# Moving weight roundings behind other ScalarE work in two stages, and spreading VectorE's convolution taps differently

## The reference

```python
# first block, its feed-forward part (D_FF = 2816)
up = einsum('bld,df->blf', h, w_up)
a, b = split(up, 2)
acc = conv_b + sum(a_pad[:, j:j + L] * conv_w[j] for j in range(3))   # 3 taps
h += einsum('blf,fd->bld', silu(acc) * b, w_down)

# each of the two layers: half a SwiGLU, this mixer, half a SwiGLU
proj = u @ w_in                      # q, k, v, a, b, g_sb, g_conv
y_sb = stick_breaking_attention(q, k, v) @ w_attn_out
x = causal_conv(a * sigmoid(b), conv_w) + conv_b      # 31 taps, 512 channels
y_conv = silu(layernorm(x)) @ w_conv_out
m = sigmoid(g_sb) * y_sb + sigmoid(g_conv) * y_conv
h += m @ w_out
```

## Time and profile before

| | |
|---|---|
| median of three runs | 1551.68 us (1550.74 to 1555.36) |
| the profiled execution, its own time | 1551.68 us |
| its span, first to last instruction | 1549.8 us |
| PE busy | 1528.6 us (99%) |
| DVE busy | 1073.2 us (69%) |
| ACT busy | 757.2 us (49%) |
| POOL busy | 406.6 us (26%) |
| mean granted TensorE clock | 0.99 |

### The profile page before, as it was taken

The page is one execution under the profiler, slowest core; times in us unless marked ns, Lnnn a source line. Parts: engine busy times, 40 slices in busy tenths (PEclk is TensorE's granted clock), DMA queues, the critical chain, the costliest instruction groups (busy, mean ns, idle before and its releaser), DMA issues.

```text
span 1549.8 us, 31398 instructions
## 1 busy us (share of the span) xinstructions
PE 1528.6 (99%) x11612; PEld 1461.0 (94%) x11612; DVE 1073.2 (69%) x1686; ACT 757.2 (49%) x1072; POOL 406.6 (26%) x158
## 2 busy tenths in 40 slices
PE   8999999999999999999999999999999999999997
PEld 7778999989999999999999999999999999999986
DVE  6333888875865768987876553755547998887754
ACT  5333665555444435447644443544444446644442
POOL 4324100053444420000034343343420000044452
PEclk9889999999999999999999999999999999999999
DMA  7213456664555554434555564455644434556662
GB/s 242 84 64 90 133 172 189 204 211 135 172 184 184 183 154 152 137 116 148 166 174 179 186 194 149 163 176 173 214 146 133 150 122 150 181 172 178 198 222 94
DMA packets 65832, 250.91 MB, mean 162 GB/s; under 512 B 7520, under 2 KB 8800, under 8 KB 65760
## 3 DMA queue, kind: packets, MB, share of 16 engines
q1 hardware_dynamic: 65760, 249.92, 51.3%
HBM read 248.84 MB, written 1.05 MB: 161 GB/s over the span
## 4 chain that ended last, share of the span: by engine, by line
PE 94%; DVE 4%; issue 1%; ACT 1%; DMA 0%; SPq 0%; DVEq 0%; ACTq 0%
PE W L1284 25%; PE W L1286 24%; PE W L1285 24%; PE W L1354 5%; PE XP L1378 5%; PE W L1353 3%; PE X L1378 2%; PE W L1322 1%; PE W L1323 1%; PE W L1324 1%; DVE wlo L730 1%; DVE scr L1143 1%; DVE proj L747 0%; DMA raw<-in_w 0%; PE X L1301 0%
## 5 line engine op out<-in xcount | busy, mean ns | idle before, releaser
L1284 PE MATMUL W<-xh,whi 128*128 128x272 f32 (+2 forms) x2416 | 702.3, 291 | 2.8 <-DVE wlo L730 1.6
L346 POOL TENSOR_TENSOR wlo<-raw,whi 128x1024 fp32r<-128x1024 f32 (+1 forms) x152 | 405.7, 2670 | 1131.2 <-ACT whi L384 1131.2
L1286 PE MATMUL W<-xh,wlo 128*128 128x272 f32 (+2 forms) x2416 | 695.7, 288 | 0.0
L1285 PE MATMUL W<-xl,whi 128*128 128x272 f32 (+2 forms) x2416 | 693.9, 287 | 0.0
L384 ACT ACTIVATE whi<-raw 128x1024 fp32r<-128x1024 f32 (+1 forms) x439 | 483.7, 1109 | 162.4 <-PE W L1286 132.3
L1284 PEld LDWEIGHTS W<-xh,whi 128*128 128x128 f32 x2416 | 458.7, 190 | 8.7 <-issue 4.9
L1285 PEld LDWEIGHTS W<-xl,whi 128*128 128x128 f32 x2416 | 458.6, 190 | 0.2
L1286 PEld LDWEIGHTS W<-xh,wlo 128*128 128x128 f32 x2416 | 458.7, 190 | 0.0
L730 DVE TENSOR_TENSOR wlo<-raw,whi 128x1024 fp32r<-128x1024 f32 (+1 forms) x285 | 370.7, 1301 | 74.3 <-ACT whi L384 73.8
L1284 PE MATMUL W<-ax,whi 128*128 128x272 f32 (+2 forms) x816 | 234.9, 288 | 1.6 <-DVE ax L1125 1.2
L1286 PE MATMUL W<-ax,wlo 128*128 128x272 f32 (+2 forms) x816 | 234.3, 287 | 0.0
(11 more groups left out here) (194 smaller groups left out, 1218.6 us busy)
## 6 DMA issues: line engine op xcount, KB each, us to landing
raw<-in_w SPq DMA_DIRECT2D x359, 512.0 KB, 3.6
raw<-in_w SPq DMA_DIRECT2D x80, 704.0 KB, 4.1
h<-in_hT SPq DMA_DIRECT2D x4, 272.0 KB, 4.8
out<-h SPq DMA_DIRECT2D x4, 256.0 KB, 2.4
scr<-in_cst SPq DMA_DIRECT2D x1, 1000.0 KB, 9.3
cst<-in_cst SPq DMA_DIRECT2D x1, 472.0 KB, 6.8
prm<-in_prm SPq DMA_DIRECT2D x1, 180.0 KB, 8.9
m<-in_meta SPq DMA_DIRECT2D x1, 64.0 KB, 8.9
```

What stands on the lines that cost most here:

```text
L346: pool.tensor_tensor(wlo[:, j, 0:cols], raw[:, j, 0:cols], whi[:, j, 0:cols].bitcast(F32), ALU.subtract).then_inc(lo_ready[j], 1)
L1284: pe.matmul(out, whi[:, j, w], mh, start=start and k == 0, stop=False, skip_group_check=True)
L1285: pe.matmul(out, whi[:, j, w], ml, start=False, stop=False, skip_group_check=True)
L1286: ins = pe.matmul(out, wlo[:, j, w], mh, start=False, stop=stop and k == len(rhs) - 1, skip_group_check=True)
```

## The change

In `tap_plan`, steps 8 to 13 get three taps each (two before), and every fourth step from step 16 on gets one (two before). The total stays 120, so the last step, 29, gets six instead of eight.

In `ffn_up` with `conv`, ScalarE does the first tap of an even slab ahead of `hi_ahead` (behind it before). Without `conv` nothing is changed.

At the end of the mixer, each `hi_ahead` between the layer norm's square root and the output projection is moved one place back: the one of slab `ga + 1`, slot 1 goes behind the four roundings of L696, slot 2 behind the large `Sigmoid` (L700), and in the loop over j the slabs of the output projection's group are rounded one turn later. VectorE's and TensorE's code is the same but for the taps.

```diff
-        room = 0 if s < 2 else 3 if s < G_GLU else 2 if s < SB_FROM else (6, 5, 2, 10)[(s - SB_FROM) % 4]
+        room = 0 if s < 2 else 3 if s < SB_FROM else (6, 5, 1, 10)[(s - SB_FROM) % 4]
...
                     for j in range(4):
                         b, c = j // 2, 2 * i + j // 2
+                        if j % 2 == 0 and conv:
+
+                            act.wait_ge(evac_done, 4 * (g + i) + j + 1)
+                            act.activation(actv[:, b, t:], gate[:, b, t:T], ACT.Identity,
+                                           scale=prm[:, bass.ds(PRM_CW1 + CONV_W * c, 1)],
+                                           bias=prm[:, bass.ds(PRM_CB1 + c, 1)]).then_inc(cv_first, 1)
                         if not first:
                             hi_ahead(g + i, j, own, nxt)
                         elif j == 2:
                             hi_ahead(g + i, 3, own, nxt)
-                        if j % 2 == 0 and conv:
-
-                            act.wait_ge(evac_done, 4 * (g + i) + j + 1)
-                            act.activation(actv[:, b, t:], gate[:, b, t:T], ACT.Identity,
-                                           scale=prm[:, bass.ds(PRM_CW1 + CONV_W * c, 1)],
-                                           bias=prm[:, bass.ds(PRM_CB1 + c, 1)]).then_inc(cv_first, 1)
                         if j % 2 == 0:
                             if conv:
                                 act.wait_ge(conv_ready, c + 1)
...
-                hi_ahead(ga, 1, K8D, K8D)
+                hi_ahead(ga, 1, K8A, K8A)
                 for c in range(CC):
                     act.wait_ge(ln_norm, CC * l + c + 1)
                     act.activation(y[:, c, :], y[:, c, :], ACT.Silu, scale=prm[:, PRM_LNG + CC * l + c:PRM_LNG + CC * l + c + 1],
                                    bias=prm[:, PRM_LNB + CC * l + c:PRM_LNB + CC * l + c + 1]).then_inc(ln_silu, 1)
-                hi_ahead(ga, 2, K8D, K8D)
                 for c in range(CC):
                     act.wait_ge(ln_silu, CC * l + c + 1)
                     act.activation(ah[:, CC + c, :], y[:, c, :], ACT.Copy).then_inc(s_hi, 1)
-                hi_ahead(ga, 3, K8D, K8D)
+                hi_ahead(ga, 2, K8A, K8A)
                 act.preload_act_table_set("sigmoid_and_others")
                 act.wait_ge(evac_done, 4 * ga)
                 act.activation(proj[:, GCV:GCV + DC, t:], proj[:, GCV:GCV + DC, t:], ACT.Sigmoid).then_inc(sig_ready, 1)
-                hi_ahead(ga + 1, 0, K8D, K8D)
+                hi_ahead(ga, 3, K8A, K8A)
                 for j in range(4):
-                    if j < 3:
-                        hi_ahead(ga + 1, j + 1, K8D, K8D)
+                    hi_ahead(ga + 1, j, K8D, K8D)
                     for m in (2 * j, 2 * j + 1):
                         act.wait_ge(mix_ready, DC * l + m + 1)
                         act.activation(ah[:, DC + m, t:], proj[:, GSB + m, t:], ACT.Copy).then_inc(mix_hi, 1)
```

More of the change, by code:

```diff
@@ L407, in group @@
                         b, c = j // 2, 2 * i + j // 2
[L408 to L411, removed]
                         if j % 2 == 0 and conv:
@@ L417, in group @@
                                            bias=prm[:, bass.ds(PRM_CB1 + c, 1)]).then_inc(cv_first, 1)
+                        if not first:
+                            hi_ahead(g + i, j, own, nxt)
+                        elif j == 2:
+                            hi_ahead(g + i, 3, own, nxt)
                         if j % 2 == 0:
```

## The result

| | before | after |
|---|---|---|
| median of 4 runs each | 1553.52 us (1550.74 to 1556.24) | 1600.23 us (1596.44 to 1604.13) |
| profiled execution, own time | 1551.68 us | 1596.78 us |
| its span | 1549.8 us | 1594.8 us |

The ratio is 1.0301 (95% interval 1.0265 to 1.0337): 46.7 us slower. The prediction said 1597 us and a span of 1595.

What follows compares the result with a forecast made beforehand. PE was taken to set the pace nearly everywhere (94% of the chain that ended last). The profiled 1551.7 us plus 32 (first feed-forward stage), 2.5 (taps) and 11 (mixer's end) gave 1597 us, range 1580 to 1610.

Steps and rivals of the forecast that it cites:

- The forecast case: Whole kernel: all three edits cost time, giving 1597 us, own range 1586 to 1606; chance 0.78.
- First tap ahead of `hi`: First feed-forward stage: even slab's `lo` starts 1.92 us later, DVE's group takes 14.51 us, above PE's 11.40; +32 us.
- The upper bound: First feed-forward stage: with no overlap the added wait is 2.3 us, a group 15.3 us, the term 40 us.
- The odd slab: Rival, first feed-forward stage: odd slab's `hi` ready without DVE's wait gives back up to 9 us; 1588 us; chance 0.08.
- the lead covers it: Rival: slabs prepared three places ahead hide the later `hi` everywhere; not slower, 1551.7 us or slightly less; chance 0.04.
- some 30 us in total: Sign, first feed-forward stage: PE's waits for `wlo` would add up to some 30 us.
- Taps: Steps 8 to 10: extra taps delay slab 11's evacuation by 1.30 us and PE's value turn; +2.5 us over two layers.
- The mixer's end: Layer norm to output projection: later `hi` delays the projection's third slab by 5.7 us; +11 us over two layers.
- The first move: Mixer's end: `hi` of slab `ga + 1`, slot 1, behind four roundings starts the convolution branch 1.28 us later on PE.
- The loop's turn: Loop at the mixer's end: DVE's turn grows from 3.36 to 5.05 us, 1.69 us more in three of four turns.
- the rival in which the end of the mixer costs nothing: Mixer's end: PE's four branch slabs outlast the loop, so only the feed-forward and tap terms count; 1586 us; chance 0.06.
- The rival of +68 us: First feed-forward stage: PE's idle time drops the clock to 1.2 GHz throughout; about 1665 us; chance 0.04.

Runs made afterwards that it cites:

- conv_only: Kernel before with only ScalarE's first-feed-forward order changed, first tap of even slabs ahead of `hi`; 1583.81 us, ratio 1.0212.
- conv_half: Kernel before with the first tap ahead of `hi` only for each group's first even slab (j = 0); 1571.97 us, ratio 1.0123.
- conv_lo_late: As conv_only, but VectorE does an even slab's `lo` behind its two taps instead of ahead of them; 1557.76 us, ratio 1.0037.
- taps_after_turn: Kernel before with the third tap only in steps 11 to 13, two in steps 8 to 10, one in every fourth later step; 1553.28 us.
- taps_four: Kernel before with four taps in each of steps 8 to 10, the rest of its tap plan unchanged; 1562.72 us.
- tail_first: Kernel before with only the `hi` of slab `ga + 1`, slot 1, moved behind the four roundings of L696; 1554.89 us.
- tail_only: Kernel before with only the moves of `hi_ahead` at the mixer's end; 1564.29 us, ratio 1.0079.
- taps_only: Kernel before with only the tap plan changed; 1553.36 us, ratio 1.0014.

## Why the prediction was right, step by step

The forecast case held: 1597 us against 1600.2, the span 1595 against 1594.8, and the three terms against the milestones of after: +32 against 32.5, +2.5 against 1.24 + 1.25 = 2.5, +11 against 5.55 + 5.46 = 11.0. What makes the profiled execution no slower than the sum is the -1.18 us ahead of the stage, where nothing is changed.

**First tap ahead of `hi`.** The path of 2.26 us from evacuation to `lo` measured 2.25, the added wait (1.92) 1.91, the group (14.51) 14.50, nine groups +30.6 (said +30.7). The first group gave 0.61 us on DVE (said up to 0.5): at 203.39 it is 1.79 us earlier than the earlier trace rows, of which 1.18 came from ahead of the stage. The last group is smaller than said: `al` starts at 347.55, so from the first row to it DVE took 144.16 us against 317.09 - 205.18 = 111.91, 32.25 more; less 30.61 that is 1.64, said 1.9. So DVE came 32.25 - 0.61 = 31.64 us later to its last `al`. PE lost 31.29 us in conv_only. It had a cover of 0.4 us that the prediction left out: the matmul that takes the last `al` up started, before, 0.45 us behind its end (317.09 + 3.27 = 320.36), and in conv_only 0.06 behind it (347.13 + 3.25 = 350.38). Before, then conv_only:

```profile
320.81 0.28 PE L1353 MATMUL W<-ax,wlo 128*128 128x256 f32 x1
```

```profile
350.44 0.39 PE L1353 MATMUL W<-ax,wlo 128*128 128x256 f32 x1
```

The other 1.25 us of after are a fall of the clock behind the stage, which was no part of the sum. So the near agreement of 32 with 32.5 is in part luck: without that fall the term was 0.7 too large. The upper bound was worked out wrongly: with no overlap the added wait is 0.67 + 0.60 + 1.06 + 0.03 - 0.34 = 2.02 us and not 2.3, which bounds the term at 34 or 35 us and not at 40; the forecast does not use it.

PE also waited once for an engine that the prediction did not name. Behind the last group the down projection began after 2.79 us of waiting for a `lo` from GpSimd, as in the row of conv_only above (conv_half's section); its `hi` stands on ACT behind a `Silu` of the last group, which waits for DVE's taps. In conv_only PE was 27.92 us late at its last matmul of this stage's slabs, 30.87 behind that wait and 31.29 behind the last `al`, the end of the path that the prediction had followed.

**The odd slab** gave nothing back: its `lo` at 223.87 waits 0.46 us for its `hi`, as its `hi` follows `Silu`. That rival is out, and so is the one in which **the lead covers it**: conv_half shows the added wait arriving whole in DVE's group. conv_lo_late shows what a real cover looks like, work of DVE's own in the place of the wait.

**PE's waits.** I wrote "some 30 us in total"; the list has 20.6. In the window from 218 to 334 us of after PE is busy 99.00 us with 769 matmuls; at the earlier trace rows's 11.40 / 96 each they are 91.3 us of pipelined work. So of 24.7 us lost there, 17.0 is idle and 7.7, or 0.24 for each of the 32 slabs, hides in busy time. At a gap it looks like this on PE:

```profile
224.35 0.28 PE L1284 MATMUL W<-xh,wlo 128*128 128x256 f32 x1
225.15 0.38 PE L1282 MATMUL W<-xh,whi 128*128 128x258 f32 x1 [0.52 <-DVE wlo L728]
```

In a row matmuls start 0.12 us apart though each is listed with 0.28; ahead of a gap the last one counts its 0.28 in full, 0.16 more, and the one behind it takes 0.38, 0.10 more (the ends of matmuls are modelled in this profile). The loss was as forecast, and I should not have expected the list of waits to hold all of it.

**Taps.** The evacuation of slab 11 came 648.74 - 616.03 - 31.36 = 1.35 us later (said 1.30):

```profile
648.74 0.43 DVE L745 TENSOR_TENSOR proj<-W,rinv 128x272 f32<-128x272 f32 x1
```

PE's turn came 1.25 later, and taps_after_turn and taps_four put the cost on steps 8 to 10 alone.

**The mixer's end.** The first move cost 1.24 (said 1.28). Slot 3's `lo` came 0.95 later (said 0.9). The loop's turn is 4.90 us, said 5.05: I took the `hi` at its length of 1.06 behind the end of the two roundings, and it overlaps them by about 0.1 (767.96 + 0.78 = 768.74 against 768.65):

```profile
767.96 0.78 ACT L705 ACTIVATE ax<-proj 128x272 fp32r<-128x272 f32 x2 [3.35 <-DVE proj L1237]
768.65 1.04 ACT L384 ACTIVATE whi<-raw 128x1024 fp32r<-128x1024 f32 x1
```

So 3 x 1.54 instead of 3 x 1.69, 0.45 us less in all. Against that the work behind the last `al` but one was taken too small: 1.4 us by the pace of 258 columns, where the rows themselves have 747.08 - 745.42 = 1.66, before and after. The two errors partly cancel: the third slab started 5.55 later (said 5.7), and the rival in which the end of the mixer costs nothing is out.

**The clock.** From 218 to 334 us of after, with PE waiting at each slab, the granted clock stayed at 1.00, the level of 2.4 GHz:

```profile
218.00:334.00 116.00, 99.00 (x769) 93.07 (x769) 76.22 (x130) 51.57 (x80) 0.00 (x0) 1.00 0.47 148
```

The rival of +68 us, the low clock through the whole stage, is out; what the clock did behind single longer waits stands in the last section. The rule of the Trainium skill that I named ("TensorE: Matmul & The Clock Gate", section "A second HAM failure mode: psum-queue depth-cycling") says that frequent short idle times can make the clock swing; the trace does not agree for waits of 0.5 to 0.7 us about every 3.6.

## What to carry to other kernels

When two engines run their instructions in order and hand work to each other, write down for each instruction of the one what it waits for and what the other does meanwhile: a delay that comes once can be covered by a lead, and one that comes in every group is covered only by the slack of the group, here 0.73 us. Before an operation that someone waits for is put behind another, ask whether the waiter has work of its own to put in the gap; where it had (conv_lo_late) 31 us became 5. Where an effect is smaller than the spread between runs, read it between two fixed points of the trace.

## What the runs showed that I had not expected

**One longer wait can cost more than itself.** The clock stayed up through a hundred microseconds of short waits, and fell behind some single waits of 1.7 to 2.8 us. Between 187 and 1500 us the twelve traces have 14 such waits of PE; in the 4 us from 0.1 us ahead of the wait's end the mean granted clock was 0.57 to 0.68 for nine of them and 1.00 for five, and waits of 1.72, 1.85 and 2.79 us are among the five. In after, behind the first feed-forward stage, PE waited 2.79 us for a `lo` from GpSimd and then ran a few microseconds at the lower level; conv_only has the same wait and no fall. Windows of after, and then of conv_only:

```profile
340.00:344.00 4.00, 1.21 (x9) 0.96 (x8) 2.05 (x1) 1.91 (x3) 3.09 (x1) 1.00 0.15 61
344.00:348.00 4.00, 4.00 (x16) 3.37 (x15) 3.00 (x7) 2.46 (x4) 0.71 (x1) 0.57 0.84 242
```

```profile
340.00:344.00 4.00, 1.23 (x7) 1.13 (x8) 2.47 (x1) 1.50 (x2) 2.67 (x1) 1.00 0.17 45
344.00:348.00 4.00, 4.00 (x25) 3.52 (x24) 3.00 (x7) 2.87 (x4) 1.12 (x1) 1.00 0.88 269
```

16 matmuls against 25 in the same place: 1.25 us (32.54 - 31.29). In conv_half, at the same place, it was up to 1.5 us, in taps_four 1.6 us in both layers, in tail_first's second layer 1.0. In the output projection of after's first layer the clock fell too, and it cost nothing, since PE waited for `al` there anyway (5.55 with it, 5.46 in the second layer). What decides whether the clock falls behind such a wait stays open.

**The spread between runs lies in one stretch.** From 34 to 146 us, where PE does many small matmuls, kernels without an edit near it differ. Windows of before, tail_only and taps_only, in this order:

```profile
34.00:146.00 112.00, 110.49 (x647) 84.99 (x647) 35.63 (x137) 34.93 (x89) 40.80 (x18) 0.89 0.27 81
```

```profile
34.00:146.00 112.00, 110.49 (x596) 84.83 (x595) 33.39 (x133) 32.97 (x85) 36.93 (x17) 0.82 0.25 76
```

```profile
34.00:146.00 112.00, 110.50 (x657) 85.04 (x656) 35.80 (x135) 34.42 (x89) 40.58 (x18) 0.91 0.28 81
```

PE is equally busy, the clock is 0.82 to 0.91, and the stage behind it starts up to 9.4 us apart (+7.72 against -1.69 in the table). That is more than the taps and one mixer's end together, and it is why tail_only's one profile is 18.8 us longer than before's while the ratio of its seven runs is worth 12.3. Ahead of 34 us the same kernels lie at most 1.1 us apart, and from 125 us to the stage no more is added than 0.2.
